# Differential attention: part of the projection two heads ahead across each head's boundary, one-pass weights, another order of the last row

## The chip, the cores and the metric

The kernel runs on one core of one Trainium2 chip. Times are device microseconds of one execution. The engines are TensorE (PE in the profile; its weight loads are PEld), VectorE (DVE), ScalarE (ACT), GpSimd (POOL) and SyncE (SP, which here only issues DMA transfers). Each engine runs its own instructions in the order in which they are written, and semaphores alone order the engines among each other.

## The reference, cut to what matters

The kernel computes one hybrid transformer block on 512 tokens of width 1024: differential attention, an mLSTM branch, cross-attention into 256 memory tokens, a gated mix, and a mixture of 32 experts. The change touches the first branch:

```python
q = rope(rms_norm(q, q_g)); k = rope(rms_norm(k, k_g))      # 8 heads, 2 components of 64
lam = exp(sum(lq1 * lk1)) - exp(sum(lq2 * lk2)) + lambda_init
s = einsum('bhcqd,bhckd->bhcqk', q_blk, k) * scale          # block of 128 queries
p = softmax(where(allowed, s, -inf))                        # keys up to the query's chunk of 64
a = p[:, :, 0] - lam * p[:, :, 1]
o = einsum('bhqk,bhkv->bhqv', a, v)                         # v has 128 columns a head
o = rms_norm(o, sub_g) * (1.0 - lambda_init)
```

## The kernel before

The stages follow one another with a barrier between them: preparation, differential attention (`stage_da`), cross-attention, mLSTM, mix, experts. `stage_da` goes through 8 heads; a head has 4 rows of 128 queries. Six heads run in a hardware loop of three turns (two heads a turn, since buffers alternate), two are written out behind it.

A head h has these steps, spread over the engines:

- Projection. For each row of head h+1 TensorE multiplies the 128 tokens by the head's 384 columns of weights for q, k and v (`proj`, 24 matmuls a row: 8 pieces of the contraction times 3, because both operands are split into a rounded high part and a low part). ScalarE takes the row out of PSUM three times (`keep_proj`: squares, q and k, v), VectorE sums the squares and makes the rotary products (`rope`, into the one buffer t1), and GpSimd makes the reciprocal root of the mean square and multiplies t1 with it (`rotate`, into qk).
- Turn of q and k. TensorE turns qk with 8 transposes into banks 6 and 7 (`turn_qk`), ScalarE copies qT and VectorE kT (`keep_qkT`, `keep_kT`).
- Scores of a row, two components (`scores`; banks 2 and 3 for even rows, 6 and 7 for odd ones), the masked and scaled maximum on VectorE (`negmax`), exponentials with their sums on ScalarE (`exps`), the weights a on VectorE (reciprocal of the sums, times lambda, and two passes over the row).
- TensorE turns a into bank 4, ScalarE copies it (aT), TensorE multiplies it with v (`pv`), ScalarE takes the output row out of PSUM with the sum of its squares (`keep_o`).
- At the head's end GpSimd makes the norm's factor (`o_rstd`), VectorE scales the output, TensorE turns it into bank 4, and VectorE copies it to y_daT with the norm's gain.
- The weights of head h+2 are split meanwhile: ScalarE rounds a fourth of the slab per row (`slab_hi`) and VectorE subtracts (`slab_lo`). The slab comes by one DMA of 1.5 MB, which SyncE issues when the projections of the head that used the buffer are done.

The order of the work is written out by hand in the four functions `body`. On TensorE, in row i of head h: scores of row i+1, projection of a row of head h+1 (rows 0, 1, and 2 and 3 in the third), pv of row i-1, turn of the weights of row i. Behind the fourth row come pv of the fourth row, the turn of q and k of head h+1, its first scores, and the turn of head h's output. I call this end of a head the boundary. In the last head, which has no head after it, four pieces of the key projection of cross-attention (`ca_keys`) take the place of the projections.

## Time and profile before

| | us |
|---|---|
| median of 3 runs (lowest, highest) | 2373.98 (2370.65, 2377.41) |
| the profiled execution's own time | 2388.6 |
| its span | 2387.0 |
| TensorE busy | 2257.5 (95%) |
| VectorE busy | 1591.8 (67%) |
| ScalarE busy | 1300.9 (55%) |
| GpSimd busy | 293.5 (12%) |

Busy times are those of the profiled execution over the whole span; the mean granted clock of TensorE in it was 0.963 of full speed. The differential attention stage begins with its first projection at 32.3 us, and the next stage's first matmul starts at 316.6 us. The expert stage, which begins behind some 1060 us, fills the rest with TensorE busy 90% or more in each slice of the page. In a line of the timeline the idle time before an instruction and what ended it stand in square brackets; a matmul of fp32 operands has two records or more, so the count behind it can be twice that of the program.

### The profile page before, as it was taken

Reading aid. Unit: us, or ns where it says so; the run is one execution under the profiler, and the core shown is the slowest. Engines: PE = TensorE matmul, PEld = TensorE weight load, DVE = VectorE, ACT = ScalarE, POOL = GpSimd, SP = SyncE. Lnnn points to the kernel's source line nnn. Section 1 sums busy time; section 2 is a strip of 40 time slices with the busy share of each in tenths; the row PEclk is TensorE's granted clock in tenths of the full one; section 3 lists DMA queues with packets and bytes.
Section 4 is the critical chain, followed back from the end, with each engine's and each line's share of the span. In section 5 each row is a group of like instructions: output and inputs, shape, how many; then the busy total and the mean of one; then the engine's idle time right before and its main releaser. Section 6 shows DMA issues by size and latency. Waiting matters only on the chain. (4 is left out here: it accounts for less than half of the span.)

```text
span 2387.0 us, 30282 instructions
## 1 busy us (share of the span) xinstructions
PE 2257.5 (95%) x10196; PEld 1809.4 (76%) x10196; DVE 1591.8 (67%) x1790; ACT 1300.9 (55%) x1526; POOL 293.5 (12%) x391
## 2 busy tenths in 40 slices
PE   5888889799999999999989999999999999999997
PEld 4777777566566688888768888888888888888885
DVE  4676744454333433434569889888889888889884
ACT  5444444233322343323337777777777777777773
POOL 1232210200122100000010110110110110110110
PEclk8998999999899999999879999999999999999998
DMA  4111033211111234334469999999999999999992
GB/s 174 36 44 53 14 128 99 102 62 53 36 36 36 90 96 132 132 97 121 196 236 353 371 365 376 358 364 369 358 369 369 367 363 368 364 365 373 362 366 88
DMA packets 89012, 515.72 MB, mean 216 GB/s; under 512 B 15108, under 2 KB 16132, under 8 KB 38184
## 3 DMA queue, kind: packets, MB, share of 16 engines
q1 hardware_dynamic: 79736, 498.14, 56.2%
q0 software_dynamic: 9216, 16.81, 2.9%
q8 instruction: 35, 0.57, 0.1%
q14 instruction: 25, 0.20, 0.0%
HBM read 508.59 MB, written 23.33 MB: 223 GB/s over the span
## 5 line engine op out<-in xcount | busy, mean ns | idle before, releaser
L1991 DVE TENSOR_TENSOR moe_lo<-moe_raw,moe_hi 128x2048 fp32r<-128x2048 f32 x382 | 855.0, 2285 | 17.5 <-ACT moe_hi L1984 14.4
L1984 ACT ACTIVATE moe_hi<-moe_raw 128x2048 fp32r<-128x2048 f32 x380 | 728.4, 1919 | 166.6 <-PE bank L2002 159.5
L2000 PE MATMUL bank<-moe_hi,moe_XTh 128*128 128x512 f32 x1024 | 403.7, 394 | 0.0
L2001 PE MATMUL bank<-moe_lo,moe_XTh 128*128 128x512 f32 x1024 | 403.6, 394 | 0.0
L2002 PE MATMUL bank<-moe_hi,moe_XTl 128*128 128x512 f32 x1024 | 403.3, 394 | 0.0
L166 ACT ACTIVATE unit_hi<-unit_raw 128x1024 fp32r<-128x1024 f32 x116 | 122.4, 1059 | 261.9 <-DMA unit_raw<-in_w_units 241.7
L172 DVE TENSOR_TENSOR unit_lo<-unit_raw,unit_hi 128x1024 fp32r<-128x1024 f32 x116 | 143.2, 1238 | 177.4 <-ACT unit_hi L166 174.8
L2002 PEld LDWEIGHTS bank<-moe_hi,moe_XTl 128*128 128x128 f32 x1024 | 193.1, 189 | 44.4
L2001 PEld LDWEIGHTS bank<-moe_lo,moe_XTh 128*128 128x128 f32 x1024 | 193.1, 189 | 44.3
L2000 PEld LDWEIGHTS bank<-moe_hi,moe_XTh 128*128 128x128 f32 x1024 | 193.7, 189 | 40.3
L2000 PE MATMUL bank<-moe_hi,moe_aTh 128*128 128x512 f32 x512 | 200.6, 392 | 1.4 <-DVE moe_aTl L2112 1.4
L2002 PE MATMUL bank<-moe_hi,moe_aTl 128*128 128x512 f32 x512 | 200.4, 391 | 0.0
L2001 PE MATMUL bank<-moe_lo,moe_aTh 128*128 128x512 f32 x512 | 200.1, 391 | 0.0
L2150 POOL DMA_INDIRECT out<-moe_y,moe_LS x32 | 51.5, 1609 | 739.8 <-ACT moe_y L2122 739.8
L2000 PEld LDWEIGHTS bank<-moe_hi,moe_aTh 128*128 128x128 f32 x512 | 96.9, 189 | 21.9 <-DVE moe_aTl L2112 1.6
L2001 PEld LDWEIGHTS bank<-moe_lo,moe_aTh 128*128 128x128 f32 x512 | 96.8, 189 | 20.3
L2002 PEld LDWEIGHTS bank<-moe_hi,moe_aTl 128*128 128x128 f32 x512 | 96.7, 189 | 20.4
L1015 PE MATMUL bank<-xnH,unit_hi 128*128 128x512 f32 x256 | 104.3, 408 | 1.1 <-PEq L649 1.1
L1535 PE MATMUL bank<-yH,unit_hi 128*128 128x512 f32 x256 | 100.0, 391 | 0.0
L1017 PE MATMUL bank<-xnL,unit_hi 128*128 128x512 f32 x256 | 99.9, 390 | 0.0
L1016 PE MATMUL bank<-xnH,unit_lo 128*128 128x512 f32 x256 | 99.8, 390 | 0.0
L1537 PE MATMUL bank<-yH,unit_lo 128*128 128x512 f32 x256 | 99.7, 389 | 0.0
(349 smaller groups left out, 3687.0 us busy)
## 6 DMA issues: line engine op xcount, KB each, us to landing
moe_raw<-in_w_moe SPq DMA_DIRECT2D x384, 1024.0 KB, 7.0
unit_raw<-in_w_units SPq DMA_DIRECT2D x116, 512.0 KB, 3.6
da_slab<-in_w_qkv SPq DMA_DIRECT2D x8, 1536.0 KB, 6.5
x_sb<-in_x SPq DMA_DIRECT2D x4, 512.0 KB, 5.1
yda_d<-y_daT SPq DMA_DIRECT2D x1, 2048.0 KB, 6.2
y_daT<-in_blocks_qk SPq DMA_DIRECT2D x1, 2048.0 KB, 8.0
y_daT<-yda_d SPq DMA_DIRECT2D x1, 2048.0 KB, 8.1
y_daT<-in_x SPq DMA_DIRECT2D x1, 2048.0 KB, 9.7
```

What stands on the lines that cost most here:

```text
L166: K.nc.scalar.activation(K.whi[:, i, :], K.wraw[:, i, :], ACT.Copy).then_inc(K.s_whi, 1)
L172: K.nc.vector.tensor_tensor(K.wlo[:, i, :], K.wraw[:, i, :], K.whi[:, i, :].bitcast(F32), ALU.subtract).then_inc(K.s_wlo, 1)
L1015: nc.tensor.matmul(out, K.whi[:, i, w], K.xnH[:, k, :], start=(k == 0), stop=False)
L1016: nc.tensor.matmul(out, K.wlo[:, i, w], K.xnH[:, k, :], start=False, stop=False)
L1017: mm = nc.tensor.matmul(out, K.whi[:, i, w], K.xnL[:, k, :], start=False, stop=(k == KT - 1))
L1535: nc.tensor.matmul(bank[:], whi[:, i, w], hi[:, x], start=(k0 + k == 0), stop=False)
L1537: mm = nc.tensor.matmul(bank[:], wl, hi[:, x], start=False, stop=(k0 + k == depth - 1))
L1984: nc.scalar.activation(HI[ring(n, pos)][:], RAW[pos][:], ACT.Copy).then_inc(s_hi, 1)
L1991: nc.vector.tensor_tensor(LO[pos][:], RAW[pos][:], HI[ring(n, pos)][:].bitcast(F32), ALU.subtract).then_inc(s_lo, 1)
L2000: nc.tensor.matmul(bank[:], xh[:, x], HI[ring][:, w], start=start and k == 0, stop=False)
L2001: nc.tensor.matmul(bank[:], xh[:, x], LO[pos][:, w], start=False, stop=False)
L2002: mm = nc.tensor.matmul(bank[:], xl[:, x], HI[ring][:, w], start=False, stop=stop and k == 3)
```

## The change

Five things change in `stage_da`, and nothing outside it but the declaration of the PSUM banks, which are now four pairs with the same eight banks inside.

1. **Projection two heads ahead.** Row 0 of head h+2 is projected at the boundary of head h, in pieces of 3, 3, 6 and 12 matmuls between the turns, the fourth pv and the scores. The other rows of head h+1 are cut in halves, the first half (FRONT) one row earlier than the second (BACK). `keep_proj` of row 0 comes in the first row of the next head as before.
2. **Scores of row 1** move from the next head's first row to the boundary, ahead of the turn of the output; that turn comes last.
3. **The fourth rotation** (row 3 of q and k) goes from GpSimd to VectorE (`rotate_last`), and q and k are turned row by row, rows 0 to 2 ahead of the fourth pv, row 3 behind it.
4. **One-pass weights and maximum.** The maxima of both components are one reduction over a pair of banks, and their masks one memset. The weights are a = E0 - (lambda l0 / l1) E1 in one pass, without the factor 1/l0, which ScalarE puts on the output row as a scale by a column (`keep_o`).
5. **Orders.** On VectorE the fourth weights come ahead of the third subtraction of the slab, and the first maximum of the next head ahead of the scaling of the output. On ScalarE `keep_o` of row i-1 comes ahead of the copy of aT of row i. The copy of the turned output goes from VectorE to ScalarE (`keep_y`), ahead of the next head's exponentials of row 1.

```diff
--- before.py
+++ after.py
...
-        self.banks = [ctx.enter_context(nc.psum_tensor(f"bank{i}", [P, 512], F32)) for i in range(8)]
+        self.pairs = [ctx.enter_context(nc.psum_tensor(f"bank{2 * i}", [P, 2, 512], F32)) for i in range(4)]
+        self.banks = [self.pairs[i // 2][:, i % 2, :] for i in range(8)]
...
-    mx, rl = sb("mx", [P, 2]), sb("rl", [P, 2])
+    mx, rl, ratio = sb("mx", [P, 2]), sb("rl", [P, TT, 2]), sb("ratio", [P, 1])
...
+    sub = sb("sub", [P, 1])
...
-    Sb = [K.banks[2:4], qkb]
+    Sb, Sp = [K.banks[2:4], qkb], [K.pairs[1], K.pairs[3]]
...
+    FRONT, BACK = range(0, KT // 2), range(KT // 2, KT)
...
-            def proj(n, par, i, first):
-                if not (first and i < 2):
+            def proj(n, par, i, ks=range(KT)):
+                if 0 in ks and not (isinstance(n, int) and n == 0 and i < 2):
                     pe.wait_ge(s_pjA, n * 4 + (i - 1))
-                if i == 0 and not first:
-                    pe.wait_ge(s_wl, n * 4 + 4)
-                for k in range(KT):
-                    if first and i == 0 and k % 2 == 0:
-                        pe.wait_ge(s_wl, k // 2 + 1)
+                for k in ks:
+                    if i == 0 and k % 2 == 0:
+                        pe.wait_ge(s_wl, n * 4 + (k // 2 + 1))
...
-                mm.then_inc(s_proj, 1)
+                if KT - 1 in ks:
+                    mm.then_inc(s_proj, 1)
...
 
-            def turn_qk(n, first=False):
-                pe.wait_ge(s_rope, n * 4 + 4)
+            def turn_qk(n, i, first=False):
+                if i < TT - 1:
+                    pe.wait_ge(s_rope, n * 3 + (i + 1))
+                else:
+                    pe.wait_ge(s_last, n + 1)
                 if not first:
                     pe.wait_ge(s_exp, START + n * 8)
                 for c in range(2):
...
+                    mm = nc.tensor.transpose(qkb[c][:, i * P:(i + 1) * P], qk[:, i, c * P:(c + 1) * P], K.ident[:])
+                if i == TT - 1:
+                    mm.then_inc(s_qkT, 1)
...
-            def body(h, par, more, more2):
-                for i in range(TT):
...
-                pv(h, par, TT - 1)
-                if more:
-                    turn_qk(h + 1)
-                    scores(h + 1, 1 - par, 0)
+            def turn_on(h):
...
+            def turn_a(h, i):
...
+
+            def body(h, par, more, more2):
+                for i in range(TT):
+                    if i in (1, 2):
+                        scores(h, par, i + 1)
+                    if i + 1 < TT:
+                        if more:
+                            if i:
+                                proj(h + 1, 1 - par, i, BACK)
+                            proj(h + 1, 1 - par, i + 1, FRONT)
+                        elif i == 0:
+                            ca_keys(1, 0)
+                            ca_keys(1, 1)
+                        else:
+                            ca_keys(i + 1, 0)
+                            if i == 1:
+                                ca_keys(2, 1)
+                    if i:
+                        pv(h, par, i - 1)
+                    turn_a(h, i)
+                    if i == 2:
+                        if more:
+                            proj(h + 1, 1 - par, 3, BACK)
+                        else:
+                            ca_keys(3, 1)
+                if more:
+                    for i in range(TT - 1):
+                        turn_qk(h + 1, i)
+                if more2:
+                    proj(h + 2, par, 0, range(0, 1))
+                pv(h, par, TT - 1)
+                if more2:
+                    proj(h + 2, par, 0, range(1, 2))
+                elif more:
+                    ca_keys(0, 0)
+                if more:
+                    turn_qk(h + 1, TT - 1)
+                if more2:
+                    proj(h + 2, par, 0, range(2, 4))
+                elif more:
+                    ca_keys(0, 1)
+                if more:
+                    scores(h + 1, 1 - par, 0)
+                    scores(h + 1, 1 - par, 1)
+                if more2:
+                    proj(h + 2, par, 0, BACK)
+                turn_on(h)
...
             for i in range(TT):
-                proj(0, 0, i, True)
-            turn_qk(0, True)
+                proj(0, 0, i)
+            for i in range(TT):
+                turn_qk(0, i, True)
+            proj(1, 1, 0, FRONT)
             scores(0, 0, 0)
+            scores(0, 0, 1)
+            proj(1, 1, 0, BACK)
             heads(pe, body, lambda: None)
 
...
-                nc.scalar.activation(osq[:], ob[:, i * P:(i + 1) * P], ACT.Square,
+                nc.scalar.activation(osq[:], ob[:, i * P:(i + 1) * P], ACT.Square, scale=rl[:, i, 0:1],
                                      accum_out=oss[:, i:i + 1]).then_inc(s_oss, 1)
-                nc.scalar.activation(on[:, i, :], ob[:, i * P:(i + 1) * P], ACT.Copy).then_inc(s_on, 1)
+                nc.scalar.activation(on[:, i, :], ob[:, i * P:(i + 1) * P], ACT.Copy,
+                                     scale=rl[:, i, 0:1]).then_inc(s_on, 1)
+
+            def keep_y(h):
+                act.wait_ge(s_yT, START + h + 1)
+                y = K.y_daT[:, h * S:(h + 1) * S] if isinstance(h, int) else K.y_daT[:, ds(h * S, S)]
+                nc.scalar.activation(y, aTb, ACT.Copy, scale=sub[:]).then_inc(s_yTe, 1)
 
...
-                    if more and projs[i]:
-                        keep_proj(h + 1, 1 - par, projs[i][0])
+                    if more and i + 1 < TT:
+                        keep_proj(h + 1, 1 - par, i)
+                    if i:
+                        keep_o(h, i - 1)
...
-                    if i:
...
-                    if more:
-                        for t in projs[i][1:]:
-                            keep_proj(h + 1, 1 - par, t)
+                    if more and i == 2:
+                        keep_proj(h + 1, 1 - par, 3)
                 keep_o(h, TT - 1)
                 if more:
                     keep_qkT(h + 1, 1 - par)
                     exps(h + 1, 0)
-
+                keep_y(h)
 
...
                 hold(K, pool, s_ss, n * 4 + (i + 1))
-                chain(rstd(pool, nc, chain, rs[:, i, :], ss[:, i, :], DH, K.half[:, 0:4]))
+                op = rstd(pool, nc, chain, rs[:, i, :], ss[:, i, :], DH, K.half[:, 0:4])
+                if i == TT - 1:
+                    op.then_inc(s_rs, 1)
+                    return
+                chain(op)
                 hold(K, pool, s_pjD, n * 4 + (i + 1))
                 if i == 0:
                     hold(K, pool, s_qkT, n)
@@ -515,12 +562,9 @@
...
             def body(h, par, more, more2):
...
+                if more:
+                    for i in range(TT):
+                        rotate(h + 1, i)
                 o_rstd(h)
 
...
-                dve.wait_ge(s_rope, n * 4 + i)
+                dve.wait_ge(s_rope, n * 3 + i)
...
+            def rotate_last(n):
+                i = TT - 1
+                dve.wait_ge(s_pjD, n * 4 + 4)
+                dve.wait_ge(s_rs, n + 1)
+                dve.wait_ge(s_qkT, n)
+                nc.vector.tensor_tensor(qk[:, i, :].rearrange("p (g d) -> p g d", g=4),
+                                        t1[:].rearrange("p (g d) -> p g d", g=4),
+                                        rs[:, i, :].unsqueeze(2).broadcast_to([P, 4, DH]), ALU.mult).then_inc(s_last, 1)
+
             def negmax(h, i, wait=True):
-                n, banks = (i + 1) * P, Sb[i % 2]
+                n, pair = (i + 1) * P, Sp[i % 2]
                 if wait:
                     dve.wait_ge(s_nm, h * 4 + i)
...
+                dve.wait_ge(s_S, h * 8 + (2 * i + 2))
+                chain(nc.vector.memset(pair[0:64, :, n - 64:n], NEG))
+                chain(nc.vector.tensor_reduce(mx[:], pair[:, :, 0:n], AX, ALU.max))
                 nc.vector.tensor_scalar(nm[i % 2][:], mx[:], -scale, None, ALU.mult).then_inc(s_nm, 1)
 
...
+            def weights(h, i):
+                n, e = (i + 1) * P, i % 2
+                dve.wait_ge(s_exp, START + h * 8 + (2 * i + 2))
+                dve.wait_ge(s_a, START + h * 4 + i)
+                chain(nc.vector.reciprocal(rl[:, i, :], l[e][:]))
+                chain(nc.vector.scalar_tensor_tensor(ratio[:], rl[:, i, 1:2], K.lamv[:, 4:5], l[e][:, 0:1], ALU.mult,
+                                                     ALU.mult))
+                dve.wait_ge(s_aT, START + h * 4 + i)
+                nc.vector.scalar_tensor_tensor(a[:, 0:n], E[e][1][:, 0:n], ratio[:], E[e][0][:, 0:n], ALU.mult,
+                                               ALU.add).then_inc(s_a, 1)
+
+            def part_lo(h, par, i, more, more2):
+                if more2:
+                    slab_lo(h + 2, par, i)
+                elif more:
+                    unit_lo(K, dve, 0, i)
+                elif i >= 2:
+                    unit_lo(K, dve, 1, i - 2)
+
             def body(h, par, more, more2):
-                for i in range(TT):
...
+                for i in range(TT - 1):
+                    negmax(h, i + 1)
+                    weights(h, i)
                     if more:
                         rope(h + 1, i)
-                    if more2:
...
+                    if i + 2 < TT:
+                        part_lo(h, par, i, more, more2)
+                weights(h, TT - 1)
+                if more:
+                    rope(h + 1, TT - 1)
+                part_lo(h, par, 2, more, more2)
+                if more:
+                    rotate_last(h + 1)
+                part_lo(h, par, 3, more, more2)
                 if more:
                     keep_kT(h + 1, 1 - par)
+                    negmax(h + 1, 0)
...
-                if more:
-                    negmax(h + 1, 0)
-                dve.wait_ge(s_yT, START + h + 1)
-                y = K.y_daT[:, h * S:(h + 1) * S] if isinstance(h, int) else K.y_daT[:, ds(h * S, S)]
-                nc.vector.tensor_scalar(y, aTb[:], K.col("g_sub"), 1.0 - LAMBDA_INIT, ALU.mult,
-                                        ALU.mult).then_inc(s_yTe, 1)
 
...
+            chain(nc.vector.tensor_scalar(sub[:], K.col("g_sub"), 1.0 - LAMBDA_INIT, None, ALU.mult))
...
+            rotate_last(0)
...
```

On TensorE, at the boundary of a head in the loop, there stood before (da_a the weights, da_aT with da_v the product with v, da_qk the turn of q and k, da_kT with da_qT scores, da_on the turn of the output):

```order
L401 MATMUL bank<-ident,da_a 128x128 x4
L381 MATMUL bank<-da_v,da_aT 128x128 x4
L361 ISA
L364 MATMUL bank<-ident,da_qk 128x128 x8
L374 MATMUL bank<-da_kT,da_qT 128x128 x2
L414 MATMUL bank<-ident,da_on 128x128 x4
L374 MATMUL bank<-da_kT,da_qT 128x256 x2
```

Now, with left out what repeats (the projections, L339 to L341, are those of row 0 two heads ahead; the three turns of rows 0 to 2 stand as one):

```order
L401 MATMUL bank<-ident,da_a 128x128 x4
...
L367 MATMUL bank<-ident,da_qk 128x128 x2
...
L339 MATMUL bank<-da_slab_hi,xnH 128x384
L340 MATMUL bank<-da_slab_lo_272,xnH 128x384
L341 MATMUL bank<-da_slab_hi,xnL 128x384
L385 MATMUL bank<-da_v,da_aT 128x128 x4
...
L378 MATMUL bank<-da_kT,da_qT 128x128 x2
L378 MATMUL bank<-da_kT,da_qT 128x256 x2
...
L392 MATMUL bank<-ident,da_on 128x128 x4
```

Six turns moved ahead of the fourth product, 24 projections stand between its start and the turn of the output (3 of them ahead of the product), and that turn moved behind both first scores.

On VectorE, from the fourth weights to the scaling of the output, there stood before:

```order
L583 SCALAR_TENSOR_TENSOR da_a<-da_E,da_rl,da_a 128x512
L536 REGISTER_ALU
L537 TENSOR_REDUCE da_ss<-da_sq 128x4
L544 TENSOR_TENSOR da_t<-da_raw,ropeC 128x256
L545 TENSOR_TENSOR da_t<-da_raw,ropeS 128x4x32
L547 TENSOR_TENSOR da_t<-da_raw,ropeS 128x4x32
L549 TENSOR_TENSOR da_t<-da_t 128x256
L568 REGISTER_ALU
L569 TENSOR_TENSOR da_slab_lo_272<-da_slab,da_slab_hi 128x768
L565 COPY da_kT<-bank 128x512
L596 REGISTER_ALU
L597 TENSOR_TENSOR da_on<-da_on,da_ors 128x512
```

Now, from behind the same rotary products:

```order
L593 TENSOR_TENSOR da_t<-da_t 128x256
L618 REGISTER_ALU
L619 TENSOR_TENSOR da_slab_lo_272<-da_slab,da_slab_hi 128x768
L600 TENSOR_TENSOR da_qk<-da_t,da_rs 128x256
...
L615 COPY da_kT<-bank 128x512
L608 ISA
L609 MEMSET bank 64x2x64
L610 TENSOR_REDUCE da_mx<-bank 128x2
L611 TENSOR_SCALAR da_nm<-da_mx 128x2
L660 REGISTER_ALU
L661 TENSOR_TENSOR da_on<-da_on,da_ors 128x512
```

The third subtraction came behind the fourth weights, the rotation (L600) between the third and the fourth subtraction (which is left out here, behind L600), and the next head's first maximum ahead of the scaling.

## Rows read from the trace of the kernel before

**Rows 1.** Windows: start:end, length, busy time per engine (instructions), granted clock, DMA.
```profile
core 0: us, PE busy (x) PEld busy (x) DVE busy (x) ACT busy (x) POOL busy (x), PEclk, DMA share, GB/s
84.30:282.00 197.70, 172.40 (x926) 148.70 (x924) 135.23 (x378) 87.20 (x296) 60.17 (x84) 0.90 0.11 40
116.90:147.20 30.30, 26.12 (x156) 22.68 (x156) 22.41 (x63) 14.36 (x50) 9.83 (x14) 1.00 0.14 52
180.30:214.40 34.10, 30.04 (x157) 25.99 (x156) 22.42 (x63) 14.39 (x50) 9.84 (x14) 0.85 0.12 46
282.00:316.60 34.60, 24.62 (x122) 18.34 (x123) 18.93 (x49) 13.07 (x44) 4.53 (x7) 0.91 0.21 62
```

**Rows 2.** Timeline of TensorE, a boundary at full clock: start, length, instruction.
```profile
118.74 1.13 PE L381 MATMUL bank<-da_v,da_aT 128*128 128x128 f32 x8 [1.20 <-ACT da_on L443]
120.92 1.09 PE L364 MATMUL bank<-ident,da_qk 128*128 128x128 f32 x8 [1.05 <-POOL da_qk L509]
122.84 0.49 PE L374 MATMUL bank<-da_kT,da_qT 64*128 64x128 f32 x4 [0.83 <-ACT da_qT L434]
123.39 0.65 PE L414 MATMUL bank<-ident,da_on 128*128 128x128 f32 x4
124.11 0.70 PE L374 MATMUL bank<-da_kT,da_qT 64*128 64x256 f32 x4
124.74 0.45 PE L339 MATMUL bank<-da_slab_hi,xnH 128*128 128x384 f32 x1
...
129.02 0.27 PE L401 MATMUL bank<-ident,da_a 128*128 128x128 f32 x1
```

**Rows 3.** Waits from 147.2 to 282: us in total, times, longest.
```profile
PE bank L401 <- DVE da_a L583: 4.5, 8, 1.0
```

**Rows 4.** The boundary in a slow head: timeline of TensorE.
```profile
184.26 1.96 PE L364 MATMUL bank<-ident,da_qk 128*128 128x128 f32 x8 [1.05 <-POOL da_qk L509]
...
184.30:189.90 5.60, 4.77 (x20) 3.27 (x20) 3.02 (x8) 1.41 (x5) 1.11 (x2) 0.50 0.16 68
```

**Rows 5.** Timeline of ScalarE and VectorE, from row 2 to row 3 of a head.
```profile
167.27 0.58 ACT L450 ACTIVATE da_E<-bank,da_nm 128x384 f32<-128x384 f32 x1 [3.27 <-DVE da_nm L561]
...
168.39 0.38 ACT L428 ACTIVATE da_sq<-bank 128x256 f32<-128x256 f32 x1
...
169.25 0.42 DVE L537 TENSOR_REDUCE da_ss<-da_sq 128x4 f32<-128x256 f32 x1 [0.84 <-ACT da_v L430]
...
170.78 0.95 DVE L569 TENSOR_TENSOR da_slab_lo<-da_slab,da_slab_hi 128x768 fp32r<-128x768 f32 x1
...
173.66 0.69 ACT L450 ACTIVATE da_E<-bank,da_nm 128x512 f32<-128x512 f32 x1 [3.01 <-DVE da_nm L561]
```

**Rows 6.** Groups by line and form, full-clock head (L874: to 520 us).
```profile
L544 DVE TENSOR_TENSOR da_t<-da_raw,ropeC 128x256 f32<-128x256 f32 x4 | 1.7, 415 | 0.0
L559 DVE TENSOR_REDUCE da_mx<-bank 128x1 f32<-128x512 f32 x2 | 1.4, 692 | 0.1
...
L583 DVE SCALAR_TENSOR_TENSOR da_a<-da_E,da_rl,da_a 128x512 f32<-128x512 f32 x1 | 0.8, 750 | 0.0
...
L559 DVE TENSOR_REDUCE da_mx<-bank 128x1 f32<-128x128 f32 x2 | 0.6, 292 | 0.1
...
L874 DVE TENSOR_REDUCE ca_mx<-bank 128x2 f32<-128x512 f32 x8 | 5.5, 691 | 20.3 <-PE bank L719 20.3
```

**Rows 7.** Timeline of GpSimd and VectorE at a fourth row.
```profile
181.56 1.13 POOL L155 TENSOR_TENSOR da_rs<-da_rs,half 128x4 f32<-128x4 f32 x1
...
182.69 0.96 DVE L569 TENSOR_TENSOR da_slab_lo<-da_slab,da_slab_hi 128x768 fp32r<-128x768 f32 x1 [0.42 <-ACT da_slab_hi L457]
182.89 1.24 POOL L509 TENSOR_TENSOR da_qk<-da_t,da_rs 128x256 f32<-128x256 f32 x1 [0.20 <-POOL da_rs L155]
```

**Rows 8.** Groups by line: copies with a column's scale, and without.
```profile
L212 ACT ACTIVATE x_sb<-x_sb,rs 128x1024 f32<-128x1024 f32 x4 | 4.3, 1136 | 2.0 <-POOL rs L155 2.0
...
L166 ACT ACTIVATE unit_hi<-unit_raw 128x1024 fp32r<-128x1024 f32 x116 | 122.4, 1059 | 261.9 <-DMA unit_raw<-in_w_units 241.7
```

**Rows 9.** Timeline of TensorE, fourth turn of the weights in the last head.
```profile
306.40 0.94 PE L401 MATMUL bank<-ident,da_a 128*128 128x128 f32 x4 [2.73 <-DVE da_a L583]
```

64 lines of the change are left out of this document (9 added, 55 removed).

## The prediction

> **What bounds the kernel now.** I read the page's shares first: TensorE is the busiest engine, and VectorE and ScalarE are far below it. The change touches the differential attention stage alone, about 32 to 316 us of the span, so what lies behind it should only shift, and the question is what a head costs there. The view by windows, cut where the fourth turn of the weights starts in a head, shows this [rows 1]. One head took 30.30 us at a granted clock of 1.00, of which TensorE worked 26.12; another took 34.10 at a clock of 0.85; the six from 84.3 to 282.0 took 197.70. VectorE is busy 22.4 us in a head and ScalarE 14.4: neither is the bound by its sum. The timeline of the full-clock head shows where TensorE idles [rows 2]: 1.20 before the fourth product with v (for ScalarE's copies), 1.05 before the turn of q and k (for GpSimd's rotation), 0.83 before the next head's scores (for qT and kT). All three stand at the boundary. The waits add VectorE's weights: 4.5 us in four heads, 1.1 each, at the second and third turns [rows 3]. Together 4.2 us. In the slow head the eight turns of q and k took 1.96 instead of 1.09, and the granted clock from there reads 0.50, the lower of its two levels, 1.2 GHz [rows 2, 4]; what came before the fall is the stretch with the gaps.
>
> **The dense work after the change.** A head keeps its 96 projection matmuls, turns and products. 24 projections in one piece take 4.28 us (124.74 to 129.02), and the first takes 0.45 where a mean of 0.18 lies between starts [rows 2]. They come in eight pieces instead of four, so up to 4 x 0.27 is added; I take 0.3, since part of a first one lies over what runs before it. TensorE needs 26.4 us. I count from T, the start of the fourth turn of the weights.
>
> **The boundary, step by step at full clock.** With rows 2: that turn to T+0.5, six of the eight turns of q and k to 1.3, three projections to 1.95, the fourth product to 3.0, three projections to 3.6, the last two turns to 3.9, six projections to 5.0, the scores of rows 0 and 1 (0.5, 0.6) to 6.1, twelve projections to 8.3, the turn of the output to 9.0 (its end 8.9), twelve projections to 11.2, the first turn of the weights. Against it:
> - The 1.20 wait. ScalarE has the third output row's square and copy by T+0.7 and the copy of aT by 1.3; TensorE comes at 1.95. Gone, 0.6 to spare.
> - The 1.05 wait. VectorE does the fourth rotation now. Its sum of squares ends at T+0.5, GpSimd's power (1.13 and three handovers of some 0.15) [rows 7] at 2.1, the rotary products at 1.7; then VectorE has the third subtraction (0.95) to 2.7 [rows 5] and the rotation, 0.42 by the multiply of the same 128x256 [rows 6], to 3.1. TensorE comes at 3.6. Gone, 0.5 to spare.
> - The 0.83 wait. VectorE has the fourth subtraction to 4.1 and kT's copy, 0.69 like the other 512-column ones, to 4.8; TensorE comes at 5.0. Nearly gone, and the tight joint: lateness above goes straight into it.
> - The output's turn waits for nothing (VectorE has scaled by 7.1, TensorE comes at 8.3). But the copy out of its bank moves to ScalarE and stands there before the exponentials of row 1, whose maximum is ready at 8.2. They start at 9.7.
>
> **The ring after it.** From there VectorE and ScalarE hand rows to each other, and one lap is in the trace [rows 5]: exponentials start at 167.27, ScalarE's copies of the projection 168.39, VectorE's sum 169.25, its subtraction 170.78, the maximum after it, exponentials again 173.66. That is 6.39 us with nothing idle on the path. The maximum takes 1.9 of it: two masks, two reductions of 0.69, a scaling. In one pass it is one mask, one reduction of 1024 elements and the scaling. The forms grow from 0.29 to 0.69 us over 384 columns, so 1024 would take 1.22, and a reduction to two maxima costs what one to a single maximum does (0.69 at 512) [rows 6]. I take 1.65 for the step and 6.15 for the lap; bounds are 6.39 (nothing saved) and 5.9 (the second fixed part of the mask, too). The lap before it, with 768 elements and shorter exponentials, 5.7. From 9.7 the laps end at 15.4 and 21.5; the exponentials of 512 columns (1.3), copies (0.86) and products (1.53) end at 25.2; reciprocal, ratio and one multiply-add of 0.75 [rows 6], where two passes stood, take 1.2. The ratio, a multiply-add of one column, is not in the trace; I take 0.2, between 0.15 and 0.4. So the fourth weights are ready at T+26.4, and TensorE comes at 26.3: ring and TensorE are level. The 1.1 us of waits for the weights go too (second ones ready 16.1, TensorE 16.8; third 22.4 and 23.1).
>
> **Two prices on top.** ScalarE's squares and copies of the output now scale by a column. A copy of 1024 columns takes 1.136 with such a scale and 1.059 without [rows 8], so 0.08 each, and two of them stand in the ring: 0.2 us with rounding.
> GpSimd's third rotation falls on VectorE's multiply-add. In the trace one of these rotations took 1.24 us and ended at 184.13, 0.48 after the end of VectorE's subtraction at 183.65 [rows 7]: it seems to have waited for it. The rotary products of the fourth row wait for the third rotation, so the tight joint can be missed by 0 to 0.5 us in each head; I take 0.4.
> The Trainium skill, SBUF — State Buffer, section "Who interferes with whom", has GpSimd and a VectorE operation with two SBUF inputs exclude each other for a whole instruction. The row agrees; by the rule the 0.4 is due in every head, without it the period would be 26.6.
> The period is then 26.4 + 0.2 + 0.4 = 27.0 us.
>
> **The sum.** Six heads: 6 x 27.0 = 162.0 against 197.7 [rows 1], -35.7. At full clock six would take 6 x 30.3 = 181.8 now, so 15.9 of that is the clock and 19.8 the waits. I take the clock to stay up, since TensorE passes the boundary with no gap over 0.4. Start: the last turns of q and k still wait for the last rotation, then twelve projections (4 us at the low clock) stand where TensorE idles 0.8 and turns to the scores; they are missing from head 0 later: the fourth turn of head 0 comes at about 81.8, not 84.3, -2.5. End: from the fourth turn of head 6 to the next stage 34.60 us now [rows 1], with a wait of 2.73 at the fourth turn of head 7 [rows 9], because VectorE subtracts a unit ahead of the weights; that goes behind them, and with the boundary's waits I get 30.8, -3.8. Total **-42.0**.
> The profiled execution took 2388.6 us with a span of 2387.0, so it would take 2346.6. The median of the runs shown is 2373.98, 14.6 lower, which the trace does not explain; from it the sum gives 2332.0. If those 14.6 are clock losses of this stage that the plain runs did not have, the gain is 27 and the time 2347: that is in the range. At nothing I cost GpSimd's lighter load (9.8 us of 30 busy) and the slab transfers: they wait for the same projection as now, and 11 us lie between it and ScalarE's first use.
>
> **Rivals.**
> - *The clock still falls.* For it: the mean over the six heads is 0.90, so it fell at most boundaries, and the boundary keeps its short turns. Against: the gaps ahead of the fall go. If the low stretch stays 8 us long, the output's turn is 3.8 late in five heads and the ring hangs on it: 2332 + 19 = 2351.
> - *The ring is the bound.* For: it is level with TensorE already, and my reduction and ratio are not in the trace. With laps of 6.39, a ratio of 0.4 and 0.2 more at each handover the period is 29.0: 2332 + 12 = 2344.
> - *It changes nothing.* New waits give back what goes, the period stays 30.3 and the clock falls as now. Against: each of the three boundary waits has its releaser done before TensorE comes. 2368 to 2374.
> - *Slower.* The output's turn stands behind 24 more projections, and all of ScalarE and VectorE's ring behind that turn. If the low clock holds from T to that turn in every head, it ends at 8.9 x 1.8 = 16.0, and 17.5 us of ring follow (8.9 to 26.4) and 0.6: 34.1 a head, 204.6 for six, no gain at the start, -3.8 at the end become -1: 2374 + 6 = 2380. It decides once that turn is 6 us late, where the period passes 32.95. Against: that would be a low stretch of 15 us of nearly gapless work, twice what the trace shows behind its gaps.
>
> **Chances.** Forecast 0.60 (own range 2325 to 2341), clock falls 0.15, ring 0.11, nothing 0.08, slower 0.06. Range: below, six heads of 26.4 (-3.6) and 5 us for the start, the end and the plain runs, 2323; above, both middle cases with a little over the clock's 2351, 2358, which leaves the last two out. A measurement of this kernel tells 0.3%, 7 us, from no change. Faster by more than that are the first three and a part of the fourth, 0.88; within it 0.07; slower 0.05.
>
> **What would show it.** Right: heads of 26.5 to 27.5 us at a clock of 1.00; no wait of TensorE for the last rotation; under 0.4 us before the first scores; row 1's exponentials straight behind the copy of the output; a small wait for VectorE at the fourth turn of the weights. Wrong: a clock of 0.85 to 0.90 per head again; laps over 6.4 us; over 0.5 us of wait for kT or the last rotation; a next stage that starts later than 280 us.

## The result, and the profile after

The changed kernel took **2332.09 us** (median of 4, 2330.74 to 2333.22), the kernel before 2374.41 beside it (4 runs, 2370.65 to 2377.41): ratio **0.9822**, interval 0.9805 to 0.9839. Forecast were 2332.0. The number came true; two of its terms did not, as the experiments show.

The windows of the changed kernel, cut like [rows 1] where the fourth turn of the weights starts in a head:

```profile
core 0: us, PE busy (x) PEld busy (x) DVE busy (x) ACT busy (x) POOL busy (x), PEclk, DMA share, GB/s
80.40:235.80 155.40, 150.99 (x925) 134.90 (x925) 117.58 (x307) 93.96 (x303) 57.18 (x79) 1.00 0.14 51
131.99:157.73 25.74, 25.09 (x155) 22.46 (x155) 19.46 (x52) 15.54 (x53) 9.41 (x14) 1.00 0.17 62
235.80:266.20 30.40, 22.48 (x122) 16.71 (x122) 16.55 (x37) 15.09 (x45) 5.51 (x7) 0.93 0.22 70
```

Six heads take 155.4 us where they took 197.7, at a clock of 1.00 throughout (2.4 GHz). A head takes 25.74, and TensorE is busy for 25.09 of it, 1.0 less than the 26.12 of [rows 1] though it has the same work. The end takes 30.4, not 34.6. The store of the stage's output, which I take as the stage's end, is issued at 266.2 us of the span; it was 316.6.

TensorE from one fourth turn of the weights (T = 183.49) to the next; what answers to [rows 2]:

```profile
183.49 0.66 PE L401 MATMUL bank<-ident,da_a 128*128 128x128 f32 x4 [0.63 <-DVE da_a L630]
183.98 0.82 PE L367 MATMUL bank<-ident,da_qk 128*128 128x128 f32 x6
185.16 1.05 PE L385 MATMUL bank<-da_v,da_aT 128*128 128x128 f32 x8
186.58 0.38 PE L367 MATMUL bank<-ident,da_qk 128*128 128x128 f32 x2
188.00 0.93 PE L378 MATMUL bank<-da_kT,da_qT 64*128 64x128 f32 x8
191.07 0.60 PE L392 MATMUL bank<-ident,da_on 128*128 128x128 f32 x4
193.63 0.27 PE L401 MATMUL bank<-ident,da_a 128*128 128x128 f32 x1
...
209.26 0.66 PE L401 MATMUL bank<-ident,da_a 128*128 128x128 f32 x4 [0.66 <-DVE da_a L630]
```

None of the three bracketed waits of [rows 2] is left: the fourth product with v (185.16), the last turns of q and k (186.58) and the scores (188.00) start without one. One wait remains, at the fourth turn. In the view of waits from 106 us to 235.8 TensorE waits for nothing but the weights: seven times, six at the fourth turns and once, for 0.52 us, at the third turn of the sixth head. The first row is TensorE's:

```profile
PE bank L401 <- DVE da_a L630: 4.4, 7, 0.7
DVE da_t L588 <- POOL da_qk L556: 0.9, 5, 0.2
```

The second row is VectorE's wait for GpSimd's third rotation, 0.2 at each boundary; nothing of it reaches TensorE. The ring of the same head, ScalarE and VectorE in order of time (what answers to [rows 5]):

```profile
191.80 0.69 ACT L487 ACTIVATE y_daT<-bank,da_sub 128x512 f32 x1 [1.54 <-PE bank L392]
192.39 0.47 ACT L494 ACTIVATE da_E<-bank,da_nm 128x256 f32<-128x256 f32 x1
198.04 0.58 ACT L494 ACTIVATE da_E<-bank,da_nm 128x384 f32<-128x384 f32 x1 [3.03 <-DVE da_nm L611]
202.81 1.23 DVE L610 TENSOR_REDUCE da_mx<-bank 128x2 f32<-128x1024 f32 x1
204.28 0.69 ACT L494 ACTIVATE da_E<-bank,da_nm 128x512 f32<-128x512 f32 x1 [2.67 <-DVE da_nm L611]
208.20 0.22 DVE L627 SCALAR_TENSOR_TENSOR da_ratio<-da_rl,lamv,da_l 128x1 f32<-128x1 f32 x1
208.45 0.75 DVE L630 SCALAR_TENSOR_TENSOR da_a<-da_E,da_ratio 128x512 f32<-128x512 f32 x1
```

The exponentials of row 1 start straight behind the copy of the output, as forecast, at T+8.90; laps of 5.65 and 6.24 follow, and the fourth weights end at 209.20, T+25.71.

Behind the loop no projection fills the boundary, and gaps stand there again. The first row is of head 6, which has no head two ahead of it, the second of the last head:

```profile
243.38 0.66 PE L392 MATMUL bank<-ident,da_on 128*128 128x128 f32 x4 [1.25 <-DVE da_on L661]
...
263.27 1.11 PE L392 MATMUL bank<-ident,da_on 128*128 128x128 f32 x4 [2.91 <-DVE da_on L661]
```

### The profile page after: what moved, and what is told of

The parts are those of the page before. It is cut to its first block, busy times and chain, and to the rows that moved or that the text cites. A ratio compares the mean times of both kernels' runs of the same rounds, so it can differ in the third digit from the quotient of the medians.

```text
span 2328.9 us, 30235 instructions
## 1 busy us (share of the span) xinstructions
PE 2224.8 (96%) x10196; PEld 1790.4 (77%) x10196; DVE 1567.8 (67%) x1695; ACT 1310.4 (56%) x1534; POOL 288.8 (12%) x383
## 4 chain that ended last, share of the span: by engine, by line
PE 49%; DVE 1%; ACT 0%; issue 0%; POOL 0%; POOLq 0%; DVEq 0%; ACTq 0%
PE bank L2060 15%; PE bank L2062 15%; PE bank L2061 15%; PE bank L2081 1%; PE bank L2071 1%; PE bank L2112 1%; PE bank L2096 0%; DVE moe_lo L2051 0%; ACT moe_hi L2044 0%; DVE moe_a L2158 0%; DVE moe_um L2152 0%; DVE moe_XTl L2136 0%; POOL out L2210 0%; ACT moe_XTh L2130 0%; DVE moe_aTl L2172 0%
```

## The experiments

Each kernel ran beside the kernel before on its own chip, and chips differ by some 0.3% (before was 2374.4 on one, 2377.8 to 2381.0 on the others). So totals are compared by their ratio to before; "a head" is the time between fourth turns of the weights in the trace.

**The kernel before once more (before_again).** No edit.

> The kernel before, unchanged, for a second profile. The first profiled execution of it took 2388.6 us, 14.6 over the median of its plain runs. Theory: that excess was a lower granted clock that varies from run to run (in the attention stage or in the mLSTM stage behind it, where the changed kernel was 8 us shorter with the same code); then this profile takes 2370 to 2378 us with a higher mean clock than 0.963. Rival: profiling itself costs the kernel before 14 us; then it takes about 2388 again at 0.963.

2374.25 us, as forecast by the theory, and on the median of the runs that I forecast from. It is one execution, and among the fast ones of its own chip, where the median was 2381.0. Its windows:

```profile
83.80:272.80 189.00, 163.68 (x927) 141.49 (x925) 135.31 (x379) 87.16 (x296) 60.15 (x84) 0.95 0.12 42
146.70:176.90 30.20, 26.11 (x157) 22.75 (x156) 22.37 (x63) 14.40 (x50) 9.83 (x14) 1.00 0.15 52
```

Six heads took 189.0 us at a mean clock of 0.95, not 197.7 at 0.90, and the store of the output is issued at 306.0, not 316.6. So most of the 14.6 us that I could not explain lay in this stage, as clock. The profile I forecast from was of an execution with an unusually low clock: 0.963 over its span, where the other 47 executions of this kernel whose clock was noted had 0.964 to 0.973, and none of them took as long. At full clock six heads take 6 x 30.2 = 181.2. In a run like this one the change therefore finds only 7.8 us of clock to win in them, and not the 15.9 of my sum; the rest of the 33.6 (189.0 less 155.4), **25.8 us, is waits and TensorE's own time**, for which I had 19.8. The stage saves 39.8 (306.0 to 266.2) of the 43.5 between these two executions. Why the stages behind it, whose code is the same, differ by the other 3.7 is not shown.

**Nothing multiplied ahead (no_ahead).** The changed kernel with the next head's first row block back beside the attention of the same head:

```
                         if more:
                             if i:
                                 proj(h + 1, 1 - par, i, BACK)
+                            else:
+                                proj(h + 1, 1 - par, 0)
...
-                if more2:
-                    proj(h + 2, par, 0, range(0, 1))
                 pv(h, par, TT - 1)
...
-                if more2:
-                    proj(h + 2, par, 0, BACK)
```

> The changed kernel with row 0 of the next head projected whole at the next head's first row, and no projection at the boundary; all else as changed. Theory (the projections at the boundary fill the gaps and so keep the clock): TensorE idles some 3.7 us a head at the boundary again, a head takes 28.8 us at full clock, which is 17 us more for six heads, and the granted clock falls at most boundaries again, up to 16 us more: 2350 to 2366, mean clock of the stage 0.90. Rival (the earlier rotation, the order and the one-pass weights do most of it, and the clock does not hang on the gaps): 2340 at a clock of 1.00.

2363.35 us, ratio 0.9929 (0.9912 to 0.9945): the gain falls from 1.8% to 0.7%, in the range of the theory, if near its upper end. TensorE at a boundary of it, in a head of 29.0 us at full clock:

```profile
115.90 0.44 PE L367 MATMUL bank<-ident,da_qk 128*128 128x128 f32 x2 [0.49 <-DVE da_qk L592]
117.42 0.96 PE L378 MATMUL bank<-da_kT,da_qT 64*128 64x128 f32 x8 [1.08 <-ACT da_qT L464]
119.52 0.66 PE L392 MATMUL bank<-ident,da_on 128*128 128x128 f32 x4 [1.14 <-DVE da_on L653]
```

The gaps come back at new places, 2.7 us of them where I expected 3.7, and with them the low clock: 0.96 over six heads (I had 0.90), 0.94 in single ones. Six heads take 179.5 us, 24.1 more than in the changed kernel: 6 x 29.0 would be 174, so some 18 of it are gaps and work and some 6 clock. The 24 projections are the filler.

**The parts alone, in the kernel before (ahead_alone, one_pass_alone, both_parts).** First the projection ahead with everything else as it was, the sixteen turns of q and k behind the fourth product, and GpSimd and VectorE untouched:

```
...
+                if more2:
+                    proj(h + 2, par, 0, range(0, 2))
                 pv(h, par, TT - 1)
+                if more2:
+                    proj(h + 2, par, 0, range(2, 4))
                 if more:
                     turn_qk(h + 1)
+                if more2:
+                    proj(h + 2, par, 0, range(4, 6))
+                if more:
                     scores(h + 1, 1 - par, 0)
+                if more2:
+                    proj(h + 2, par, 0, range(6, 8))
```

> The kernel before with row 0 of head h+2 projected at the boundary of head h (two pieces of 6 matmuls around the fourth product, 6 behind the turn of q and k, 6 behind the first scores), and nothing else of the change. Theory: the boundary is filled and the clock stays up, but VectorE's and ScalarE's ring (two-pass weights and maxima, the third and fourth subtraction of the slab ahead of what TensorE waits for) then bounds a head at 29.7 us, with 3 to 4 us of wait for the weights: 6 x 0.6 and the clock's share, 2355 to 2368. Rival (filling the boundary is nearly the whole gain): 2340 or less.

Then the one-pass weights and maxima alone, with ScalarE's scale; of the edit only the weights are shown:

```
...
-                    chain(nc.vector.tensor_scalar(a[:, 0:n], E[e][1][:, 0:n], rl[:, 1:2], None, ALU.mult))
-                    nc.vector.scalar_tensor_tensor(a[:, 0:n], E[e][0][:, 0:n], rl[:, 0:1], a[:, 0:n], ALU.mult,
+                    nc.vector.scalar_tensor_tensor(a[:, 0:n], E[e][1][:, 0:n], ratio[:], E[e][0][:, 0:n], ALU.mult,
...
```

> The kernel before with the one-pass maximum and one-pass weights (and ScalarE's scale of the output row) alone. Theory: only the waits for weights go, 1.0 us a head, and some of the 2.7 in the last head; the boundary keeps its three gaps and its low clock: 2365 to 2369. Rival (VectorE's passes were the bound all along): 2355 or less.

Then both of these edits together, still in the old order:

> The kernel before with the projection ahead and the one-pass weights together, and nothing of the new order: all sixteen turns of q and k stay behind the fourth attention product, GpSimd rotates the fourth row block, the fourth weights stand behind two slab subtractions, the output's copies behind aT on ScalarE, y on VectorE. Each of the two parts alone gave nothing that could be told (ratios 1.000 and 0.999). Theory (the new order is the third part that is needed; of the ring it takes off what the one-pass weights do not): a head of the projection ahead alone took 30.75 us, and one pass for two took 1.2 us a head off the ring of the changed kernel, so heads of 29.0 to 29.6 us, still with a wait of 1 us or more ahead of the fourth turn of the weights; ratio to before 0.993 to 0.998. Rival (the two parts are super-additive by themselves, the order only tidies): heads of 26.5 to 27.5 us, ratio 0.980 to 0.986.

| kernel | us | ratio to before | clock, six heads |
|---|---|---|---|
| ahead alone | 2381.21 | 1.0004 (0.9990 to 1.0017) | 0.94 |
| one pass alone | 2379.02 | 0.9986 (0.9969 to 1.0003) | 0.93 |
| both, old order | 2375.02 | 0.9980 (0.9971 to 0.9990) | 0.94 |
| the whole change | 2332.09 | 0.9822 (0.9805 to 0.9839) | 1.00 |

Each gives nothing that can be told, and together they give 0.2%. The rest of the 1.8% needs **the new order**: with the one-pass weights it gives 0.7% (no_ahead), with the projection ahead 1.5% (two_pass, below). The order without either part was not run. Three of its pieces are taken back one by one below: the place of the third subtraction, that of the scores, and the fourth rotation on VectorE. The early turns of q and k and ScalarE's order of copies are not tested apart. My numbers for the first two (2355 to 2368, 2365 to 2369) and the head of the third (29.0 to 29.6) missed low; the ratio of the third is in its range.

With the one pass alone TensorE's waits for the weights fall from 6.3 us in six heads (before_again) to 0.9, as expected. But six heads take 189.6 and not 189.0: 1.1 of it is waited more at the fourth product, and the clock is 0.93 and not 0.95, so TensorE is busy for 167.8 and not 163.7. TensorE at the fourth turn, ahead alone:

```profile
177.42 1.12 PE L400 MATMUL bank<-ident,da_a 128*128 128x128 f32 x4 [2.52 <-DVE da_a L589]
...
180.22 1.05 PE L380 MATMUL bank<-da_v,da_aT 128*128 128x128 f32 x8
```

and with both parts:

```profile
174.55 0.91 PE L381 MATMUL bank<-da_v,da_aT 128*128 128x128 f32 x6 [1.50 <-ACT da_on L450]
177.46 0.66 PE L401 MATMUL bank<-ident,da_a 128*128 128x128 f32 x4 [2.00 <-DVE da_a L588]
...
179.52 2.02 PE L381 MATMUL bank<-da_v,da_aT 128*128 128x128 f32 x8
```

The boundary's own gaps are gone, but the ring of ScalarE and VectorE is late: 2.52 us at the fourth turn, 1.16 at the third product. A head is still 30.75 us: 25.1 of work, 3.7 of waits, and some 2 of clock, which with these gaps falls again at each boundary. With one pass the wait is 0.52 shorter, and yet a head is 30.75 again: 0.34 more is waited at the third product for ScalarE's copies of the output, which this order puts behind aT's, and the clock now falls a little later, over the fourth product (2.02 us where it took 1.05). I read from this that boundary and ring both stood near 30 us, so that removing one shows the other. From the fourth turn to the first matmul behind that product it is 3.74 us, with the first part alone 3.61. Why 0.52 less and 0.34 and 0.13 more nearly cancel is open; no run here separates them.

**What the one pass is worth beside the new order (two_pass).** The changed kernel with two maxima and two passes for the weights. The second pass is a plain addition, since ScalarE divides by the sum; the kernel before had a multiply-add there.

```
-                nc.vector.scalar_tensor_tensor(a[:, 0:n], E[e][1][:, 0:n], ratio[:], E[e][0][:, 0:n], ALU.mult,
-                                               ALU.add).then_inc(s_a, 1)
+                chain(nc.vector.tensor_scalar(a[:, 0:n], E[e][1][:, 0:n], ratio[:], None, ALU.mult))
+                nc.vector.tensor_tensor(a[:, 0:n], E[e][0][:, 0:n], a[:, 0:n], ALU.add).then_inc(s_a, 1)
```

> The changed kernel with the maximum as two masks and two reductions, and the weights in two passes over the row (the ratio as changed). Theory (the ring of ScalarE and VectorE bounds a head, TensorE waits 0.63 us for the fourth weights): each of two laps grows by 0.25 and the fourth weights by 0.4 to 0.5, so TensorE's wait grows to 1.6 us and a head from 25.75 to 26.7: 2338. Rival (TensorE is the bound, the wait is slack of something else): the growth is hidden but for a few tenths, 2332 to 2334.

2345.9 us, ratio 0.9854 (0.9834 to 0.9875). Heads take 26.97 us, 1.2 more, and three turns wait for the weights:

```profile
149.38 0.44 PE L401 MATMUL bank<-ident,da_a 128*128 128x128 f32 x2 [0.18 <-DVE da_a L633]
156.06 0.55 PE L401 MATMUL bank<-ident,da_a 128*128 128x128 f32 x3 [0.36 <-DVE da_a L633]
160.39 0.66 PE L401 MATMUL bank<-ident,da_a 128*128 128x128 f32 x4 [1.01 <-DVE da_a L633]
```

The three waits are 1.55 together; I had 1.6, all of it at the fourth turn. The theory of the ring holds; the size was 0.25 a head low.

**The third subtraction ahead of the fourth weights again (third_lo_first).**

```
-                    if i + 2 < TT:
-                        part_lo(h, par, i, more, more2)
+                    part_lo(h, par, i, more, more2)
                 weights(h, TT - 1)
                 if more:
                     rope(h + 1, TT - 1)
-                part_lo(h, par, 2, more, more2)
```

> The changed kernel with VectorE's third slab subtraction (0.95 us) ahead of the fourth weights, as in the kernel before. Theory (ring): the fourth weights and TensorE's fourth turn come 0.95 us later in each head, the boundary gets nothing back since the last rotation is not what it waits for: 6 x 0.95, 2337 to 2338. Rival (slack): under 2334.

2349.37 us, ratio 0.9877 (0.9852 to 0.9901). I had expected 2337 to 2338. The wait at the fourth turn grows by 1.2, not by 0.95, and heads to 26.96; 0.15 of the difference is the ratio's step, 0.38 us long for 0.22 while GpSimd's rotation runs beside it.

```profile
160.10 0.65 PE L401 MATMUL bank<-ident,da_a 128*128 128x128 f32 x4 [1.88 <-DVE da_a L630]
```

One instruction of 0.95 us in another place costs the stage 11.1 us (its store at 277.3). Five heads give 6.0 of it. In the sixth the clock fell behind the 1.89 us gap at 214.01, and it took 29.8 (26.5 in the changed kernel); behind gaps of 1.86 to 1.89 in the heads before it had not, and no run shows why. The last took 25.7 and not 22.0, with a wait of 2.0. Less 1.8 at the start and the end, that is the 11.1. The profiled execution was the fastest of the four, 2340.82; the others took 6 to 12 us more at a lower clock. The six turns of q and k behind that gap, 0.82 long in the changed kernel:

```profile
214.72 1.49 PE L367 MATMUL bank<-ident,da_qk 128*128 128x128 f32 x6
```

**The ring's start (scores_behind).** The scores of row 1 behind the output's turn, where they stood before:

```
                     scores(h + 1, 1 - par, 0)
-                    scores(h + 1, 1 - par, 1)
                 if more2:
                     proj(h + 2, par, 0, BACK)
                 turn_on(h)
+                if more:
+                    scores(h + 1, 1 - par, 1)
```

> The changed kernel with the scores of the second row block behind twelve projection products and the turn of the output at the boundary, where they stood in the kernel before, in place of ahead of them; nothing else is changed. With T the start of the fourth turn of the weights: their bank would be written by T+8.5, VectorE's MEMSET, maximum over 512 and TENSOR_SCALAR (0.17, 0.69, 0.17 us) end at T+9.6, and the exponentials of row 1 start there and no longer at T+8.9. Theory (the ring starts with these scores and has only the 0.66 us at the fourth turn as slack in TensorE's favour): everything behind comes 0.7 to 0.8 later, the wait at the fourth turn is 1.3 to 1.5, heads of 26.4 to 26.6 us, 4 to 6 us more in all, ratio to before 0.984 to 0.985. Rival (ScalarE's copy of y, which waits for the turn of the output in either order, sets the start): heads stay at 25.8, ratio 0.982.

2340.01 us, ratio 0.9846 (0.9800 to 0.9891: its runs spread widely, and the interval overlaps that of the changed kernel). The trace is what decides. Its head from T = 186.52:

```profile
186.52 0.66 PE L401 MATMUL bank<-ident,da_a 128*128 128x128 f32 x4 [0.63 <-DVE da_a L631]
...
196.13 0.47 ACT L495 ACTIVATE da_E<-bank,da_nm 128x256 f32<-128x256 f32 x1 [1.08 <-DVE da_nm L612]
...
208.36 0.61 PE L385 MATMUL bank<-da_v,da_aT 128*128 128x128 f32 x4
209.03 0.55 PE L401 MATMUL bank<-ident,da_a 128*128 128x128 f32 x3
...
213.00 0.66 PE L401 MATMUL bank<-ident,da_a 128*128 128x128 f32 x4 [0.65 <-DVE da_a L631]
```

and the window of this head:

```profile
186.52:213.00 26.48, 25.77 (x154) 22.59 (x154) 19.47 (x52) 15.63 (x52) 9.42 (x14) 1.00 0.14 55
```

The exponentials start at T+9.61, 0.71 later, and a head takes 26.5, 0.73 more. **The ring's start moves the head one for one**, the cleanest result of the study. The laps behind it are those of the changed kernel (5.66 and 6.23). The wait at the fourth turn, though, stayed 0.65, where I expected 1.3 to 1.5. The turns before it start at T+10.48, 16.15 and 22.51, and were at 10.14, 15.68 and 21.79, and none shows a wait in TensorE's row. The first 0.34 of this is no lateness of the ring: the first turn's weights hang on row 0, whose exponentials start at T+5.97 in both. It is TensorE's own: the same work in this order, with the scores in two groups, takes that much longer. The rest is the ring's, and it hides under the ends of the rows before: the third turn starts 0.67 us behind the third product here and 0.44 in the changed kernel, where the product's row is 0.61 long. In the changed kernel:

```profile
204.84 0.61 PE L385 MATMUL bank<-da_v,da_aT 128*128 128x128 f32 x4
205.28 0.55 PE L401 MATMUL bank<-ident,da_a 128*128 128x128 f32 x3
```

That TensorE is busy for 25.77 in this window, and for 25.1 in the changed kernel, is both of these together.

**GpSimd rotates the fourth row too (pool_rotates).** As in the kernel before, `rotate_last` gone.

> The changed kernel with the fourth rotation back on GpSimd. Theory: it waits for the power and then for VectorE's fourth subtraction, so the last turn of q and k starts about 4.1 us behind the fourth turn of the weights instead of 3.1, the first scores 0.7 later, and all behind it: 6 x 0.7, 2336 to 2337, with a wait of TensorE for GpSimd of some 1 us in each head. Rival (the boundary has slack enough): 2332.

2330.9 us, ratio 0.9800 (0.9776 to 0.9825), heads of 25.82: the rival was right, and I had the conflict of the two engines wrong. Who rotates the fourth row does not matter in this order. GpSimd and VectorE there, and VectorE's two subtractions by the view of that tile (durations in ns, least, median, most):

```profile
186.91 0.73 POOL L549 TENSOR_TENSOR da_qk<-da_t,da_rs 128x256 f32<-128x256 f32 x1 [0.20 <-POOL da_rs L156]
```
```profile
186.22 2.24 DVE L612 TENSOR_TENSOR da_slab_lo<-da_slab,da_slab_hi 128x768 fp32r<-128x768 f32 x2
```
```profile
L612 DVE TENSOR_TENSOR da_slab_lo<-da_slab,da_slab_hi x2: 951/1160/1369, 186.2 to 187.1; 128x768 fp32r<-128x768 f32 x2
```

I had let GpSimd wait behind both subtractions. It waits for the running one only: that one takes 0.95 us and ends at 187.17, GpSimd is done at 187.64, and the second takes 1.37, 0.42 more, just a rotation's length on VectorE [rows 6]. Five heads of this trace have the same lengths (0.73, and 2.23 to 2.24 for the two subtractions). The Trainium skill, SBUF — State Buffer, section "Who interferes with whom", has the two exclude each other for a whole instruction, by order of issue: the trace agrees, but the lock changes hands between two instructions, so the price is one instruction, not a queue of them.

**The last wait (y_behind, lo_in_idle, both).** Two ways to shorten the ring further. ScalarE's exponentials of row 1 ahead of its copy of the output:

```
...
                     exps(h + 1, 0)
+                    exps(h + 1, 1)
                 keep_y(h)
...
```

> The changed kernel with ScalarE's exponentials of the next head's row 1 ahead of its copy of the turned output. In the trace they are ready at 191.15 and start at 192.39, behind that copy. Theory (ring): the ring starts 0.7 to 1.2 us earlier, which takes away TensorE's wait of 0.63 for the fourth weights and no more, since TensorE has 25.1 us of work: a head takes 25.1 to 25.2, 2328 to 2329. Rival (the first lap waits for ScalarE's copies of the row 0 projection or the slab anyway): 2332.

And VectorE's first two subtractions between weights and rope, each a row later, in time in which VectorE waits for ScalarE (the third already stood behind the fourth weights and stays; the expectation counts it with them):

```
                     weights(h, i)
+                    if i:
+                        part_lo(h, par, i - 1, more, more2)
                     if more:
                         rope(h + 1, i)
-                    if i + 2 < TT:
-                        part_lo(h, par, i, more, more2)
                 weights(h, TT - 1)
```

> The changed kernel with each of VectorE's first three slab subtractions put between the weights of a row and the rope of a row (in time in which VectorE waits for the projection's copy), in place of behind the rope. Theory (a head's only wait, 0.66 us at the fourth turn of the weights, is the tail of VectorE's ring; what is moved off VectorE's stretch ahead of its next maximum shortens the lap): the wait falls to 0.1 to 0.3, heads from 25.78 to 25.2 to 25.4 us, the attention stage 2.5 to 3.5 us shorter, total 2328 to 2330 where the changed kernel stands at 2332 (ratio to before 0.979 to 0.981). Rival (ScalarE's exponentials set the lap, VectorE has slack beside them): heads stay at 25.7 to 25.8, total 2332, ratio 0.982.

> The changed kernel with both: the subtractions in VectorE's idle time, and ScalarE's exponentials of the second row ahead of its copy of y. Theory (TensorE's own work, 25.1 us a head, is the floor, and either edit alone nearly reaches it): heads of 25.0 to 25.2 us, the wait at the fourth turn under 0.1 us, the stage 3 to 4 us shorter than in the changed kernel, total 2328, ratio 0.979 to 0.980. Rival (the two laps add their savings below the 25.1 us): heads under 24.8 us, total 2325 or less, ratio 0.978 or less.

| kernel | a head, us | wait at the fourth turn | store of the stage | total, ratio to before |
|---|---|---|---|---|
| changed | 25.76 | 0.65 | 266.2 | 2332.09, 0.9822 |
| y_behind | 25.25 | 0.20 | 264.0 | 2331.14, 0.9796 (0.9774 to 0.9817) |
| lo_in_idle | 25.15 | none | 261.7 | 2331.18, 0.9789 (0.9768 to 0.9811) |
| both | 25.14 | none | 261.5 | 2327.66, 0.9788 (0.9765 to 0.9810) |

A window of one head, of both edits:

```profile
130.60:155.74 25.14, 25.05 (x157) 22.32 (x155) 19.37 (x51) 15.79 (x51) 9.28 (x13) 1.00 0.17 63
```

TensorE is busy for 25.05 of 25.14 us. This is the floor of a head with this work in this order; the theory given for both edits together holds, and once one is in, the other adds next to nothing. The stage is 4.7 us shorter, where I expected 3 to 4, and 4.5 by lo_in_idle alone, where I expected 2.5 to 3.5. In the total that does not show beyond doubt: the intervals touch that of the changed kernel, and what lies behind the stage differs by several us from run to run (both: 2322.7 to 2334.2). "Both" has the lowest median of all kernels here, by 3 us, but it was not timed directly against the changed one. How little 0.2% says between such sets of runs shows in pool_rotates: its ratio is 0.9800, below the 0.9822 of the changed kernel, with heads that are 0.06 us longer.

## Why the prediction was right, and where it was not

Its steps, on the scale T of the prediction, beside the head of the trace above:

| step | predicted | measured |
|---|---|---|
| fourth product starts | 1.95 | 1.67 |
| last turns of q and k | 3.6 | 3.09 |
| scores | 5.0 | 4.51 |
| output's turn | 8.3 | 7.58 |
| exponentials of row 1 | 9.7 | 8.90 |
| laps | 5.7, 6.15 | 5.65, 6.24 |
| reduction of 1024, ratio | 1.22, 0.2 | 1.23, 0.22 |
| fourth weights ready | 26.4 (26.6 with scales) | 25.71 |
| TensorE's own head | 26.3 to 26.4 | 25.14 (both) |
| a head | 27.0 | 25.76 |

**What was right.** The three boundary waits went, for the reason given (no_ahead brings them back), and the clock stayed at its upper level. Ring and TensorE are indeed level: 25.7 against 25.1. The laps came out within 0.1 us each, the unseen operations within 0.02. The ring from T+9.7 to T+26.4, 16.7 us of it, measured 16.8 (8.90 to 25.71).

**The dense work was mis-sized.** The step "they come in eight pieces instead of four, so up to 4 x 0.27 is added; I take 0.3" has the wrong sign. TensorE's busy time went from 26.12 to 25.09. TensorE's timeline at a boundary of the kernel with both edits shows why:

```profile
181.31 0.82 PE L367 MATMUL bank<-ident,da_qk 128*128 128x128 f32 x6
181.88 0.42 PE L339 MATMUL bank<-da_slab_hi,xnH 128*128 128x384 f32 x1
...
182.49 1.05 PE L385 MATMUL bank<-da_v,da_aT 128*128 128x128 f32 x8
183.30 0.42 PE L339 MATMUL bank<-da_slab_hi,xnH 128*128 128x384 f32 x1
...
184.14 0.44 PE L367 MATMUL bank<-ident,da_qk 128*128 128x128 f32 x2
184.33 0.42 PE L339 MATMUL bank<-da_slab_hi,xnH 128*128 128x384 f32 x1
```

In this trace a group costs its full length only where nothing follows it. Six turns are 0.82 long and the next work starts 0.57 after them, the fourth product 1.05 and 0.81, two turns 0.44 and 0.19. I had counted groups by the length of their rows, and paid 0.3 more for the pieces. Together that made TensorE's head 1.2 us too long. An estimate from these rows agrees: in the kernel before, four or five groups of a head stood ahead of a wait and showed their last 0.25 us, which is 1.0 to 1.2.

**So the ring started early.** The output's turn stood at 7.58 and not 8.3, so the exponentials came 0.8 earlier; scores_behind shows that this passes into a head one for one. It is the same error a second time, not another, and it is the term that made the period too long: 27.0 less this 0.8 and the 0.4 below is 25.8.

**The 0.4 for GpSimd was not due.** The conflict itself came as forecast: the third rotation ended 0.48 behind VectorE's multiply-add. But VectorE's rotary products of the fourth row waited only 0.2 for it in every head, and neither the last turns nor the scores waited. pool_rotates shows how little a longer conflict does here. The size of a scaled copy on ScalarE was right (0.08 forecast, 0.09 measured, below); that two of them cost the ring 0.2 no run shows apart.

**The clock was counted too high, and the two errors cancelled.** Against the profile before, six heads gave -42.3 where I had -35.7, the start -3.9 where I had -2.5, and the end -4.2 where I had -3.8: -50.4, not -42.0. But I put the sum onto the median of the plain runs, which did not have the low clock of that profile. before_again is an execution of the same time as their median: against it the change gave -33.6, -3.4 and -2.8, together -39.8, and 3.7 behind the stage. I named this case in one sentence of the sum, and priced it at 2347. With the 8 us of clock that this run had, my terms would have given 27.0 (189.0 less 162.0), 2.5 and 3.8, that is 33.3 of the 43.5 measured. The 10.2 that are missing are 6.6 in the heads, 0.9 at the start and 3.7 behind the stage, which I had at nothing, less 1.0 too much at the end. So a clock term too high by 8 stood against a head too long by 1.2, and a hit within 0.1 us is partly luck.

**The rivals.** The clock did not fall in the six heads. "The ring is the bound" is true in its mechanism, at 25.7 and not 29.0. The two that end at no change or slower needed new waits; none came.

## What to carry to other kernels

Before you count a part of a change alone, look at what is next: here the boundary and the ring both ended near 30 us a head, and the parts gave 0.0%, 0.1% and, together, 0.2%, the whole 1.8%. Where TensorE gets dense, take a short group from its start to the start of the next, not by the length of its row. And before a clock loss is booked as gain, profile the kernel before a second time: one execution had 16.5 us of it in this stretch (197.7 against 181.2 at full clock), the next 7.8.

## What the runs showed of the hardware

- ScalarE's copies and squares of 128x128 with a column as scale take 0.39 us and without 0.30, in groups of 20 and 17, changed kernel and the kernel before:

```profile
L481 ACT ACTIVATE da_on<-bank,da_rl 128x128 f32<-128x128 f32 x20 | 7.8, 388 | 0.0
```
```profile
L443 ACT ACTIVATE da_on<-bank 128x128 f32<-128x128 f32 x17 | 5.1, 300 | 0.0
```

  The Trainium skill, ScalarE: Activation LUTs, section "What ACT_TABLE_LOAD costs", has some 93 ns for each such operand; the trace agrees with 88.
- A short wait need not show in the listing of TensorE's waits: in scores_behind the third turn starts 0.67 us behind the third product, 0.23 later than in the changed kernel, with no wait listed, since the product's row is 0.61 long. The only wait listed stays 0.65.
- GpSimd and VectorE, both with two inputs in SBUF, take turns by the instruction: in pool_rotates 0.42 us is added to one subtraction of 0.95, nothing to its neighbour.
